# Third block's feed-forward in two phases, with seven block products per 2x2 blocks and the block sums on GpSimd

## The reference

```python
D_MODEL, SEQ, D_FF_3 = 1024, 1024, 4096
def channel_mlp(h, w1, b1, w2, b2):
    return jnp.square(jax.nn.relu(h @ w1 + b1)) @ w2 + b2

def deepnorm_update(x, y, gate, g, b):
    return layer_norm_3(ALPHA_3 * x + gate * y, g, b)
...
        x_new = deepnorm_update(x, y_l, g1, ln1_g[l], ln1_b[l])
        x_new = deepnorm_update(x_new, channel_mlp(modulate(x_new, sh2, sc2), w1[l], b1[l], w2[l], b2[l]),
                                g2, ln2_g[l], ln2_b[l])
```

## Time and profile before

| | us |
|---|---|
| median of 3 runs | 3772.07 |
| lowest, highest run | 3766.03, 3773.8 |
| span of the profiled execution | 3772.8 |
| of it the last stage, from its first matmul at 2923.92 | 848.9 |
| PE busy in the span | 3631.5 (96%) |
| DVE busy in the span | 2237.2 (59%) |
| ACT busy in the span | 1233.3 (33%) |
| POOL busy in the span | 198.5 (5%) |

### The profile page before, as it was taken

The page is one execution under the profiler, slowest core; times in us unless marked ns, Lnnn a source line. Parts: engine busy times, 40 slices in busy tenths (PEclk is TensorE's granted clock), DMA queues, the critical chain, the costliest instruction groups (busy, mean ns, idle before and its releaser), DMA issues. The chain is left out here.

```text
span 3772.8 us, 42367 instructions
## 1 busy us (share of the span) xinstructions
PE 3631.5 (96%) x17008; PEld 2942.7 (78%) x17008; DVE 2237.2 (59%) x3016; ACT 1233.3 (33%) x1789; POOL 198.5 (5%) x221
## 2 busy tenths in 40 slices
PE   8999999999998999999999999988998999999997
PEld 7977778888886877668788888867986778888885
DVE  4487577777777897454456555456355664444445
ACT  3344432222224413543322222244323462322223
POOL 0000000000003101230000000022100000000000
PEclk9999999999999999999999999999998999999999
DMA  3102111111111112120132222211222101111111
GB/s 126 45 1 90 34 45 51 51 51 50 40 51 56 62 56 53 39 90 34 45 119 94 90 90 90 89 62 46 63 59 94 41 25 65 45 45 45 45 60 53
DMA packets 68149, 225.29 MB, mean 60 GB/s; under 512 B 5565, under 2 KB 18237, under 8 KB 62706
## 3 DMA queue, kind: packets, MB, share of 16 engines
q1 hardware_dynamic: 67954, 222.58, 16.8%
HBM read 200.34 MB, written 13.70 MB: 57 GB/s over the span
## 5 line engine op out<-in xcount | busy, mean ns | idle before, releaser
L1262 PE MATMUL psum<-mixer_r,pairs_r 128*128 128x512 f32 x2016 | 793.8, 394 | 8.6 <-DVE gemm_input_r L1693 5.3
L1264 PE MATMUL psum<-mixer_r,pairs_r 128*128 128x512 f32 x2016 | 785.9, 390 | 0.0
L1263 PE MATMUL psum<-gemm_input_r,pairs_r 128*128 128x512 f32 x2016 | 785.8, 390 | 0.0
L1301 PE MATMUL psum<-hidden_r,pairs_r 128*128 128x512 f32 x1216 | 478.8, 394 | 13.0 <-DVE residual L1751 6.1
L1302 PE MATMUL psum<-hidden_r,pairs_r 128*128 128x512 f32 x1216 | 475.3, 391 | 0.0
L1303 PE MATMUL psum<-hidden_r,pairs_r 128*128 128x512 f32 x1216 | 475.2, 391 | 0.0
L1757 DVE TENSOR_TENSOR residual<-residual,psum 128x512 f32<-128x512 f32 x560 | 361.7, 682 | 171.4 <-PE psum L1303 144.3
L1262 PEld LDWEIGHTS psum<-mixer_r,pairs_r 128*128 128x128 f32 x2016 | 379.7, 188 | 93.3 <-issue 9.2
L1263 PEld LDWEIGHTS psum<-gemm_input_r,pairs_r 128*128 128x128 f32 x2016 | 379.7, 188 | 82.4 <-issue 4.1
L1264 PEld LDWEIGHTS psum<-mixer_r,pairs_r 128*128 128x128 f32 x2016 | 379.3, 188 | 79.2
L1699 DVE TENSOR_TENSOR pairs_r<-pairs,pairs_r 128x2048 fp32r<-128x2048 f32 (+1 forms) x108 | 223.4, 2070 | 276.5 <-ACT pairs_r L1444 276.5
(11 more groups left out here) (566 smaller groups left out, 5851.0 us busy)
## 6 DMA issues: line engine op xcount, KB each, us to landing
pairs<-in_w_up SPq DMA_DIRECT2D x38, 1024.0 KB, 6.9
pairs<-in_w SPq DMA_DIRECT2D x32, 1024.0 KB, 5.3
pairs<-in_w_down SPq DMA_DIRECT2D x16, 1024.0 KB, 5.2
norm_a<-in_w_ada SPq DMA_DIRECT2D x12, 1024.0 KB, 4.9
norm_b<-in_w_ada SPq DMA_DIRECT2D x12, 1024.0 KB, 5.0
pairs<-in_w_down SPq DMA_DIRECT2D x22, 512.0 KB, 3.5
pairs<-in_w_in SPq DMA_DIRECT2D x10, 1024.0 KB, 5.3
weight_slots<-in_w_in SPq DMA_DIRECT2D x9, 1024.0 KB, 4.9
```

Of the source, the lines that this page charges most:

```text
L1262: pe.matmul(out, w_hi[:, at], c.MR[:, k, halves[n]], start=k == 0, stop=False)
L1263: pe.matmul(out, w_hi[:, at], c.HR[:, k, halves[n]], start=False, stop=False)
L1264: mm = pe.matmul(out, w_lo[:, at], c.MR[:, k, halves[n]], start=False, stop=k == KT - 1)
L1301: pe.matmul(bank, hi, hid(0, ch, n, kd), start=kd == 0, stop=False)
```

## The change

`chain_stage` is replaced for the third block by `phased_stage`. The projection with w_out, the norms and the first three chunks of the up projection (EARLY = 3, as before 12 units of 24 matmuls) stay. The rest works in two phases.

**Up phase.** The other 13 chunks (PAIRS) are each one 2x2 block problem: two row blocks of w1 (4 tiles of 128 deep each) by two halves of positions. Instead of 8 block products it makes 7 (a Winograd form of Strassen's method), each 4 x 3 = 12 matmuls, 84 in all where 96 stood. The sums of the activations' blocks are made once by VectorE; the four sums of weight blocks of each pair (128x512 each) are made by GpSimd (`block_parts`) from a slab in `stage_rows`, then ScalarE rounds them (`round_blocks`, `round_sums`) and VectorE makes the lo parts (`low_blocks`). Results are put together from products: ScalarE copies some out of PSUM (`copy`), VectorE adds others (`add`). The finished hidden rows go to DRAM (`hidden_rows`, 64 writes of 256 KB).

**Down phase.** 28 of the 32 hidden tiles are taken in five stretches of 4, 6, 6, 6 and 6 tiles (DEPTHS = 2, 3, 3, 3, 3 per block). In each stretch there are 4 groups (output tiles j and j + 4), 20 groups in all (GROUPS), each of 7 products of h x 3 matmuls (h = 2 or 3): 42 or 63 matmuls where 48 or 72 stood. The blocks of hidden rows are read back from DRAM (`load_block`), four sums of them are made by GpSimd for each stretch (`operand_sums`, 128x1024 for the first, 128x1536 after), and each of the 7 operands is rounded and split (`round_operand`, `low_operand`). For each group a slab of w2 (512 or 768 KB) is loaded (`load_down`), four sums of 128x256 or 128x384 are made by GpSimd (`down_sums`), ScalarE rounds (`round_down`) and VectorE splits (`low_down`). There are 2 places for these slabs. The last 4 hidden tiles are done as before, 192 matmuls (`down_tail_part`).

**Residual.** ALPHA*x is no longer put into X ahead. The norm's result goes to DRAM and comes back one tile at a time in groups 8 to 15 (`add_residual`, 128x1024, VectorE). In the first stretch ScalarE writes the first product of each bank to X (`touch`), all other products are drained by VectorE (`drain`, 7 per group after the first stretch).

The core of the diff:

```diff
+DEPTHS = (2, 3, 3, 3, 3)
+BANK_OF = (0, 1, 0, 2, 0, 2, 0)
+OPENS = (True, True, False, True, False, False, False)
+UP_PLACE = (0, 1, 5, 4, 3, 2, 6)
+DOWN_PLACE = (0, 1, 5, 4, 2, 3, 6)
...
+def phased_stage(c, w_out, up, down, down_tail, first, last, mix_gate, bias, gate, x_affine, mix_src, offsets, store, prefetch=()):
+    N, EARLY = 16, 3
+    PAIRS = N - EARLY
...
+            for i in range(PAIRS):
+                keep(i, "11")
+                if i == 0:
+                    for m in range(4):
+                        sp.wait_ge(kept[m], 48)
+                    for name in ("B11", "B21"):
+                        load_block(0, name)
+                if i + 2 < PAIRS:
+                    sp.wait_ge(w_sums, 4 * (i + 2))
+                    sp.wait_ge(w_lo, SLABS + 3 * (i + 1) + 2)
+                    load_stage(i + 2)
+                if i == PAIRS - 1:
+                    sp.wait_ge(products, UP + 7 * (PAIRS - 1))
+                    load_block(0, "B22")
+                    load_block(0, "B12")
+                    load_down(0)
+                keep(i, "22")
+                keep(i, "21")
+                if i == PAIRS - 1:
+                    sp.wait_ge(products, UP + 7 * PAIRS)
+                    load_down(1)
+                keep(i, "12")
...
+            for g in range(GROUPS):
+                q, j = divmod(g, 4)
+                if g:
+                    sp.wait_ge(products, DOWN + 7 * g)
+                    if g + 1 < GROUPS:
+                        load_down(g + 1)
+                if j == 0:
+                    sp.wait_ge(b_lo, 7 * (q + 1))
+                if q + 1 < CHUNKS_ and j < 2:
+                    for name in (("B22", "B12"), ("B11", "B21"))[j]:
+                        load_block(q + 1, name)
...
+            def product(bank, r, h, w_high, w_low, hi, lo):
+                b_high, b_low = block(*hi[r], h), block(*lo[r], h)
+                for k in range(h):
+                    at = slice(k * P, (k + 1) * P)
+                    pe.matmul(bank, w_high[:, at], b_high[:, k, :], start=OPENS[r] and k == 0, stop=False, skip_group_check=True)
+                    pe.matmul(bank, w_high[:, at], b_low[:, k, :], start=False, stop=False, skip_group_check=True)
+                    mm = pe.matmul(bank, w_low[:, at], b_high[:, k, :], start=False, stop=k == h - 1, skip_group_check=True)
+                return mm
...
+            def down_group(g):
+                q, j = divmod(g, 4)
+                h = depth(g)
+                pe.wait_ge(w_lo, SLABS + 3 * PAIRS + 2 * g + 1)
+                for r in range(7):
+                    if r == 2:
+                        pe.wait_ge(w_lo, SLABS + 3 * PAIRS + 2 * g + 2)
+                    if j == 0:
+                        pe.wait_ge(b_lo, 7 * q + r + 1)
+                    if g == 0 and r == 0:
+                        pe.wait_ge(copied, all_up + 4 * (PAIRS - 2) + 4)
+                        pe.wait_ge(added, 3 * (PAIRS - 2) + 3)
+                    if g == 1 and r == 0:
+                        pe.wait_ge(copied, all_up + 4 * PAIRS)
+                        pe.wait_ge(added, 3 * PAIRS)
+                    if g >= 2 and r in (0, 1, 3):
+                        drained(g - 2, {0: 6, 1: 1, 3: 5}[r])
+                    if r in (2, 4, 5, 6):
+                        drained(g, {2: 0, 4: 2, 5: 3, 6: 4}[r])
+                    product(PS[:, 3 * ((g + 1) % 2) + BANK_OF[r], :], r, h, down_high(g, DOWN_PLACE[r]), down_parts(g, DOWN_PLACE[r]),
+                            DOWN_HI, DOWN_LO).then_inc(products, 1)
...
+            for i in range(PAIRS):
+                if i + 1 < PAIRS:
+                    round_blocks(i + 1)
+                copy(i, "11", 0)
+                if i + 1 < PAIRS:
+                    round_sums(i + 1)
+                else:
+                    round_down(0, True)
+                copy(i, "21", 2)
+                if i == PAIRS - 1:
+                    round_operand(0, 0)
+                    round_operand(0, 1)
+                    round_operand(0, 2)
+                    round_down(0, False)
+                copy(i, "22", 3)
+                if i == PAIRS - 1:
+                    for r in range(3, 6):
+                        round_operand(0, r)
+                copy(i, "12", 6)
+            round_operand(0, 6)
+            for g in range(GROUPS):
+                q, j = divmod(g, 4)
+                if q == 0:
+                    touch(g, 0)
+                if g + 1 < GROUPS and (g or q):
+                    round_down(g + 1, True)
+                if j == 3 and q + 1 < CHUNKS_:
+                    round_operand(q + 1, 0)
+                if q == 0:
+                    touch(g, 2)
+                if j == 3 and q + 1 < CHUNKS_:
+                    round_operand(q + 1, 1)
+                    round_operand(q + 1, 2)
+                if q == 0:
+                    touch(g, 3)
+                if g == 0:
+                    round_down(1, True)
+                if g + 1 < GROUPS:
+                    round_down(g + 1, False)
+                if j == 3 and q + 1 < CHUNKS_:
+                    round_operand(q + 1, 3)
+                    round_operand(q + 1, 4)
+                    round_operand(q + 1, 5)
+                if q == 0:
+                    touch(g, 6)
+                if j == 3 and q + 1 < CHUNKS_:
+                    round_operand(q + 1, 6)
...
+            def down_sums(g):
+                pool.wait_ge(w2_landed[g % 2], 16 * (g // 2 + 1) + (0 if g % 2 else 16 * PAIRS))
+                part = lambda place: down_parts(g, place, 1, parts)
+                pool.tensor_tensor(part(4), part(0), part(2), ALU.subtract).then_inc(w_sums, 1)
+                pool.wait_ge(w_sums, 4 * PAIRS + 4 * g + 1)
+                pool.tensor_tensor(part(2), part(2), part(3), ALU.add).then_inc(w_sums, 1)
+                pool.wait_ge(w_sums, 4 * PAIRS + 4 * g + 2)
+                pool.tensor_tensor(part(5), part(2), part(0), ALU.subtract).then_inc(w_sums, 1)
+                pool.wait_ge(w_sums, 4 * PAIRS + 4 * g + 3)
+                pool.tensor_tensor(part(6), part(1), part(5), ALU.subtract).then_inc(w_sums, 1)
+            def operand_sums(q):
+                raw = lambda name: raw_block(q, name)
+                for name in b_landed:
+                    pool.wait_ge(b_landed[name], 16 * (q + 1))
+                pool.tensor_tensor(raw("T3"), raw("B22"), raw("B12"), ALU.subtract).then_inc(b_sums, 1)
+                pool.wait_ge(b_sums, 4 * q + 1)
+                pool.tensor_tensor(raw("T1"), raw("B12"), raw("B11"), ALU.subtract).then_inc(b_sums, 1)
+                pool.wait_ge(b_sums, 4 * q + 2)
+                pool.tensor_tensor(raw("T2"), raw("B22"), raw("T1"), ALU.subtract).then_inc(b_sums, 1)
+                pool.wait_ge(b_sums, 4 * q + 3)
+                pool.tensor_tensor(raw("T4"), raw("B21"), raw("T2"), ALU.subtract).then_inc(b_sums, 1)
+            for i in range(PAIRS):
+                block_parts(i)
+            pool.wait_ge(w_lo, SLABS + 3 * PAIRS)
+            operand_sums(0)
+            down_sums(0)
+            for g in range(GROUPS):
+                if g + 1 < GROUPS:
+                    down_sums(g + 1)
+                if g % 4 == 2 and g // 4 + 1 < CHUNKS_:
+                    operand_sums(g // 4 + 1)
...
+            for g in range(GROUPS):
+                q, j = divmod(g, 4)
+                switch = j == 3 and q + 1 < CHUNKS_
+                if g in READD:
+                    add_residual(g)
+                for r in range(7):
+                    if (g, r) in drain_at:
+                        drain(g, r)
+                    if switch and r:
+                        low_operand(q + 1, r - 1)
+                    if g + 1 < GROUPS and r == 2:
+                        low_down(g + 1, True)
+                    if g + 1 < GROUPS and r == 3:
+                        low_down(g + 1, False)
+                if switch:
+                    low_operand(q + 1, 6)
...
-            (3, lambda f: chain_stage(c, "w_out_3", "w1_3", "w2_3", 16, mix_gate=ada(16), bias="b1_3", gate=ada(40),
+            (3, lambda f: phased_stage(c, "w_out_3", "w1_3", "w2_3", "w2_t_3", mix_gate=ada(16), bias="b1_3", gate=ada(40),
```

685 lines of the change are left out of this document (681 added, 4 removed).

## The result

The changed kernel takes 3823.95 us (median of 4 runs, 3819.82 to 3827.35). The kernel before, measured beside it, takes 3772.94. The ratio is 1.0132 with a 95% interval of 1.0116 to 1.0148, so the change costs 1.3%, some 51 us. The profiled execution has a span of 3822.6 us, 49.8 more than the one of before.

What follows compares the result with a forecast made beforehand. PE was taken as the bound, at 0.2262 us a matmul. The terms -73.3 + 17.6 + 90 + 7 = +41 on the span of 3772.8 gave 3814, less 0.7, rounded to 3812 us; range 3793 to 3838, chance 0.55.

Steps and rivals of the forecast that it cites:

- Matmuls removed: Last stage: 324 fewer matmuls (2748 for 3072 in the feed-forward) at 0.2262 us each, -73.3 us.
- Pairs hide their work: Up phase, pairs 0 to 11: the other engines' work fits into 19.0 us a pair; PE waits some 1 us at the first.
- Last pair: End of the up phase: loads, GpSimd sums and rounding delay the copy that products 6 and 7 need, +17.6 us with clock drop.
- Down phase: The 20 groups: late slab chains, drains behind splits and work left over at changes of stretch cost +90 us in all.
- 70 us of waits in 40 to 50 places: Down phase, profile after: PE's waits named after DVE drains, some 70 us in 40 to 50 waits, granted clock below 0.95.
- my walk without any drop in the short waits: Bound on the sum: with no clock drop at the short waits the change costs +33 us instead of +41.
- The ends: Tail's weight split +3, last norm +5 and a mean's wait +2, pair 0 +1, an early wait gone -4: together +7 us.
- The -4 for a wait of 5.3: Wait of L1262: most of its 5.3 us goes, since ACT no longer makes ALPHA*x ahead of the early units, -4 us.
- Engines shutting each other out: DVE instructions with two SBUF inputs wait for a running POOL sum, drains do not; sum +41 us with it, +18 without.
- the milder rival (3790): Engines do not shut each other out for whole instructions; third groups cost +1.7, -22 of the sum, 3790 us; chance 0.12.
- the sign to look for: Third group of a stretch, profile after: the small lo part should take over 3 us, not 0.95.
- GpSimd busy 210 us: Last stage, profile after: POOL should be busy about 210 us with its sums.

## Why the prediction was right

The time was forecast at 3812 and measured at 3824 (3822.6 in the profile, where the sum said 3814), inside the forecast range of 3793 to 3838. The terms one by one:

- **Matmuls removed, -73.3.** 324, at the same 0.2262: the twelve pairs take 19.04 each. Right.
- **Pairs hide their work, +1 at the first.** PE waited 0.9 us once. Right, though GpSimd's sums were slower than I read from the earlier trace rows: two of the four of 512 took 2.27 and 1.63 on average where I had 1.30, because VectorE's splits lie beside them. The 19 us had room for it.
- **Last pair, +17.6.** Measured 36.8 - 19.04 = +17.8. The chain is the one forecast; the wait named was ScalarE's copy, 13.1 us in two pieces where I had said once, some 12. The first piece, 4.6 us, I had missed: the copy of "21" stands behind the rounding of the slab's first part, which waits for the slab to land.
- **Down phase, +90.** Measured 358.7 - 266.0 = +92.7. Ordinary groups 15.7 to 16.3 (forecast 15.9), third ones 21.2 to 21.3 (21.8), fourth ones 20.0 to 20.6 (20.6 to 21.3), first ones of the later stretches 15.7, 20.6, 20.7, 18.5 (16.1, 20.4, 20.4, 17.3). The first stretch was worse: its four groups lost 26.6 us, not 21.2, and most of the difference lies in the third, which took 19.2, not 15.9, at a clock of 0.77. The later stretches lost some 2.7 us less than forecast, so part of the closeness of 92.7 to 90 is luck: two errors of opposite sign.

```profile
3404.20:3423.40 19.20, 12.05 (x44) 9.42 (x43) 10.57 (x5) 4.90 (x7) 15.35 (x8) 0.77 0.10 27
```

- **What the +90 is made of was off.** I wrote of 70 us of waits in 40 to 50 places. There are 61.7 in 34. The other 31 us are matmuls at the lower clock and restarts; in my walk without any drop in the short waits 8 us would have gone, so I had the clock's share about four times too small and the waits somewhat too large, and that these two errors nearly cancel is luck as well. About 130 of the 1176 matmuls start over 0.3 us after the one before without a wait between them, and these alone lose 23.5 us. One such stretch, behind a wait of 3.46 us:

```profile
3523.08 0.77 PE L2359 MATMUL psum<-mixer_r,parts_r 128*128 128x512 f32 x1 [3.46 <-DVE residual L2794]
3523.64 0.63 PE L2360 MATMUL psum<-gemm_input_r,parts_r 128*128 128x512 f32 x1
3524.07 0.63 PE L2361 MATMUL psum<-mixer_r,parts_r 128*128 128x512 f32 x1
```

Their starts are 0.43 apart, where 0.23 is usual; that is the lower level, 1.2 GHz. It goes on for nine more matmuls.

- **The ends, +7.** The tail's weight split made PE wait 3.14 us (forecast 3). The last norm's mean waited 6.46 where it had waited 1.60 (forecast +5). The -4 for a wait of 5.3 that would go was wrong: it is the first product of the stage, which waits for VectorE's split of its input, and it still waits 5.0. I had put it down to ScalarE's later work without looking at which matmul it was. The rest of the stage, pair 0 included, taken as what the other terms leave (45.7 + 73.3 - 17.8 - 92.7), came to +8.5. It was not followed wait by wait.
- **Engines shutting each other out.** The step on the earlier trace rows holds, and with it the choice against the milder rival (3790): the small lo part of a third group takes 4.13 us, where the sign to look for was over 3. The rule of the Trainium skill's page "GPSIMD Engine Reference", section 8 (Key points), names VectorE instructions with two SBUF inputs. The rows here agree: drains, which read PSUM, kept their 0.74.
- **GpSimd busy 210 us.** It was 247.3, by the same mutual delay. This had no price of its own in the sum.

Of the 12 us between forecast and measurement 4.1 lie ahead of the stage, where nothing was changed, and 4.4 in it (2.7 in the down phase, 1.5 at the ends, 0.2 in the last pair). The other 3.5 say nothing of the kernel: the profiled span of the changed kernel lies 1.4 below its median, I had taken off 0.7 for the span of the kernel before, and 3814.1 - 0.7 is 3813.4 and not 3812.

## What to carry to other kernels

Fewer matmuls pay only where the other engines' chains fit into the shorter step. Here the up phase fitted and kept its saving (19.04 us a pair); the down phase saved 38 us by count and gave back 93, and some 65 of these came back with another order, earlier loads and another place for the operand sums, with no less work. Before giving sums to an idle engine, see which engine it shuts out: in this kernel a sum of 1536 cost less on the busier VectorE (1.75 us) than on GpSimd (3.5 to 5.3, with VectorE's splits standing still beside it). And in an in-order queue what another engine waits for must stand ahead of work that only has to be done some time: that was worth 45 us.

## What the runs showed of the hardware that I had not expected

The delay works both ways and adds up when both engines run chains: GpSimd's third operand sum took 5.28 us in three of the four stretches, the first 3.47, and two slab sums of 256 at the last pair took 1.58 instead of 0.72. The stages ahead of the change, the same in all versions, ended at times that differ by 11.7 us between the profiled executions (first pair at 3104.7 to 3116.4), while repeated runs of one version lie 4 to 15 us apart; so a version's time can be off by several us for reasons that have nothing to do with its edit, and effects of that size were read from the changed section alone. With one profiled execution of each version the traces can't tell a difference between versions from one between executions of the same version; the cause stays open.
